# The last two weight halves of a feed-forward part's second matrix, used together, one row block after the other

## The reference, cut to what matters

```python
D_FF = 2816
def swiglu(h, w_in, w_out):
    gate, up = jnp.split(h @ w_in, 2, axis=-1)
    return (jax.nn.silu(gate) * up) @ w_out

for l in range(2):
    x = x + 0.5 * swiglu(rms_norm(x, ffa_norm[l]), ffa_w_in[l], ffa_w_out[l])
    h = rms_norm(x, mix_norm[l])
    ...                                   # three mixing branches, x = x + (...) @ w_out
    x = x + 0.5 * swiglu(rms_norm(x, ffb_norm[l]), ffb_w_in[l], ffb_w_out[l])
return x
```

## Time and profile before

| | us |
|---|---|
| median of 3 runs | 2600.22 |
| the profiled execution | 2601.14 |
| span of its trace | 2599.0 |
| TensorE busy | 2471.0 (95%) |
| GpSimd busy | 1019.3 (39%) |
| ScalarE busy | 900.9 (35%) |
| VectorE busy | 857.8 (33%) |

### The profile page before, as it was taken

How to read it: one execution, slowest core, us unless ns; L and a number is a source line. 1 busy time by engine, 2 the same in 40 slices (tenths; PEclk the granted TensorE clock), 3 DMA queues, 4 the chain that set the end, 5 groups by cost and what they waited for, 6 DMA issues and landing times. The chain is left out here.

```text
span 2599.0 us, 37017 instructions
## 1 busy us (share of the span) xinstructions
PE 2471.0 (95%) x15110; PEld 1780.1 (68%) x15110; DVE 857.8 (33%) x1424; ACT 900.9 (35%) x1342; POOL 1019.3 (39%) x428
## 2 busy tenths in 40 slices
PE   8879999999999999979999999999999999999999
PEld 3544444333443334438998899899899888998998
DVE  0332122111221122233117756421231277564211
ACT  1211211111111111134446752444444467424443
POOL 0000000000000000016887653788878876537886
PEclk9979999999999999989999999999999999999999
DMA  9139999999999999944554332555555543325554
GB/s 362 69 121 413 428 428 428 428 428 428 428 428 428 428 428 428 388 170 154 185 183 153 132 110 75 177 183 187 188 171 186 185 149 129 111 74 170 176 184 143
DMA packets 95392, 653.66 MB, mean 252 GB/s; under 512 B 10593, under 2 KB 12817, under 8 KB 69297
## 3 DMA queue, kind: packets, MB, share of 16 engines
q1 hardware_dynamic: 95280, 652.06, 65.1%
HBM read 650.96 MB, written 1.06 MB: 251 GB/s over the span
## 5 line engine op out<-in xcount | busy, mean ns | idle before, releaser
L546 POOL TENSOR_TENSOR w_lo<-raw,w_hi 128x1024 fp32r<-128x1024 f32 (+2 forms) x424 | 1019.1, 2427 | 1565.8 <-ACT w_hi L540 1565.7
L1882 PE MATMUL bank<-ring,scratch 128*64 128x512 f32 x3072 | 686.1, 596 | 29.1 <-DMA ring<-in_expert_units 26.8
L540 ACT CAST w_hi<-raw 128x1024 fp32r<-128x1024 f32 (+2 forms) x424 | 420.3, 1038 | 436.1 <-PE bank L561 428.1
L559 PE MATMUL bank<-hT_hi,w_hi 128*128 128x256 f32 x1984 | 567.3, 286 | 4.1 <-DVE hT_lo L650 4.1
L561 PE MATMUL bank<-hT_hi,w_lo 128*128 128x256 f32 x1984 | 564.2, 284 | 0.0
L560 PE MATMUL bank<-hT_lo,w_hi 128*128 128x256 f32 x1984 | 564.2, 284 | 0.0
L1882 PEld LDWEIGHTS bank<-ring,scratch 128*64 128x64 f32 x3072 | 209.6, 137 | 457.0 <-issue 386.3
L559 PEld LDWEIGHTS bank<-hT_hi,w_hi 128*128 128x128 f32 x1984 | 383.8, 193 | 6.2 <-issue 4.3
L560 PEld LDWEIGHTS bank<-hT_lo,w_hi 128*128 128x128 f32 x1984 | 383.8, 193 | 0.8
L561 PEld LDWEIGHTS bank<-hT_hi,w_lo 128*128 128x128 f32 x1984 | 383.5, 193 | 0.0
L2050 DVE TENSOR_TENSOR scratch<-bank,scratch 128x512 f32<-128x512 f32 x64 | 44.3, 692 | 606.4 <-PE bank L1896 602.5
(11 more groups left out here) (315 smaller groups left out, 2742.2 us busy)
## 6 DMA issues: line engine op xcount, KB each, us to landing
ring<-in_expert_units SPq DMA_DIRECT2D x192, 2048.0 KB, 20.6
raw<-in_layer_halves SPq DMA_DIRECT2D x408, 512.0 KB, 4.1
ring<-in_first_units SPq DMA_DIRECT2D x6, 2048.0 KB, 24.0
scratch<-in_ple_units SPq DMA_DIRECT2D x2, 2048.0 KB, 9.8
raw<-in_layer_halves SPq DMA_DIRECT2D x8, 424.0 KB, 3.3
scratch<-in_norm_gains SPq DMA_DIRECT2D x6, 512.0 KB, 6.0
raw<-in_layer_halves SPq DMA_DIRECT2D x4, 384.0 KB, 3.7
const<-in_const SPq DMA_DIRECT2D x1, 1184.0 KB, 7.5
```

What stands on the lines that cost most here:

```text
L540: k.nc.scalar.copy(k.w[0][i % SPLIT_SLOTS][:, at], k.raw[n % RAW_SLOTS][:, 0:at.stop - at.start]).then_inc(k.shared("weights_hi"), 1)
L546: k.nc.gpsimd.tensor_tensor(k.w[1][i % SPLIT_SLOTS][:, at], k.raw[n % RAW_SLOTS][:, 0:at.stop - at.start], k.w[0][i % SPLIT_SLOTS][:, at], ...
L559: nc.tensor.matmul(out, lhsT[0], rhs[0], start=start, stop=False)
L1882: last = nc.tensor.matmul(b[g * SL:(g + 1) * SL, :], lhsT[:, c, :], w[:, c, g, :], start=start and c == 0, stop=stop and c == 3)
```

## The change

For unit 5, TensorE takes the second half of out 4 ("ahead") and the half of out 5 together. For row block 0 it multiplies the two chunks of ahead into both banks, then the two chunks of out 5 into (0,0) and (0,1), each of which is released when complete; then the same for row block 1. `half_used` for ahead is raised after ahead's products for row block 1. Unit 4 does only its first half. The number of matmuls, their operands and the order of the semaphore's counts are the same.

```diff
     if u == FFN_OUT_UNITS - 1:
+        ahead = weights_pe(k, pe, (f"ffn{n}", "out", u - 1, 1), D)
         w = weights_pe(k, pe, (f"ffn{n}", "out", u, 0), D)
         for t in range(NT):
+            for i in range(2):
+                for v in range(2):
+                    last = product(ahead, 4 * u - 2 + i, i, t, v)
+            if t == 1:
+                last.then_inc(k.shared("half_used"), 1)
             for v in range(2):
                 for i in range(2):
                     last = product(w, 4 * u + i, i, t, v)
                 last.then_inc(out[t, v][1], 1)
         return
-    for h in range(2):
+    for h in range(1 if u == FFN_OUT_UNITS - 2 else 2):
         w = weights_pe(k, pe, (f"ffn{n}", "out", u, h), D)
```

## The result

The changed kernel is slower. Its median of four executions is 2620.19 us (2617.47 to 2621.55) against 2601.01 us for the kernel before; the ratio is 1.0072, 95% interval 1.0054 to 1.009, so 14 to 23 us. In a second comparison it came out at 1.0064 (1.005 to 1.0078). The forecast of 2616.7 us and its range of 2611 to 2623 hold. The profiled execution took 2619.06 us, 17.9 more than the one before.

A forecast was written before the change was run, and what follows sets the result against it. The prediction took TensorE to bound the kernel, so its standing still counts. Boundaries 12.15, program's end 1.33 and clock 3.0 sum to 16.5 us, taking the median from 2600.22 to 2616.7 us, range 2611 to 2623.

The forecast's parts named there:

- The stall: Before ahead's products, TensorE waits for act_lo of in 10: 1.33 us at each of four places, 5.3 us alone.
- the forecast's lower bound of 0.78 us: Wait before ahead's products if act_lo did not hold and only out 5's split at 1355.52 counted: 0.78 us.
- The late slot: Ahead's slot is freed later, so ScalarE's cast and the norm move 4.05 us at three boundaries, 12.15 us including the wait.
- The clock: Longer TensorE idle before the three boundaries' transposes lowers its clock: 1.6, 1.0 and 0.4 us, 3.0 in all.
- The sum: Whole program: 12.15 + 1.33 + 3.0 = 16.5 us slower, median 2616.7 us.
- The early release: VectorE takes block 0 out 1.39 us earlier, then waits for (1,0) before any variance: gain nothing.
- The rival that named the two points from which it decides: At three boundaries, early release pulls block 0's norm forward 3.2 us each: 9.5 us faster, 2590.7 us; chance 0.02.
- That only the stall counts: ScalarE's lateness is covered, boundaries move only with TensorE's wait: 4 x 1.33 = 5.3 us, 2605.5 us; chance 0.05.
- That the clock is lost at every boundary as at the start of the layers: Low TensorE clock costs 3 us at each of three boundaries: 13.5 + 3 x 3 = 22.5 us, 2622.7; chance 0.12.

The follow-up runs named there:

- the run with both mendings: Changed kernel with waits for out 5's inputs behind ahead's products for row block 0, and the second next half's cast behind block 0's squares: 1.0035.
- the second trace: The changed kernel itself, nothing altered, run and traced once more beside the experiments: 1.0064 against the kernel before.
- the run with the norm ahead: Changed kernel with waits where needed, VectorE doing block 0's variance and rows before taking out (1,0), ScalarE's cast behind block 0's root: 0.9994.
- the late release alone: Kernel before with only half_used of ahead raised 13 matmuls later: 1.0044, 11.4 us.

## Why the prediction was right

**The stall: right.** 1.33 us were forecast at each of four places. Measured from act_lo, (1,0) goes out 1.38, 1.36 and 1.36 us later, and the last piece 13.72 - 12.35 = 1.37. Alone it moves the first boundary by 1.36, and it goes when the waits move. What makes act_lo so late is itself a hold: it takes 2.45 us while GpSimd subtracts, and where GpSimd stood still the kernel before did the same instruction in

```profile
2426.98 0.69 DVE L820 TENSOR_TENSOR act_lo<-scratch,act_hi 128x512 fp32r<-128x512 f32 x1 [0.69 <-ACT act_hi L805]
```

At that length the act_lo that starts at 1353.62 would end at 1354.31, before TensorE's 1354.89; out 5's split would then have been the later input, the forecast's lower bound of 0.78 us. No run tried this.

**The late slot: right in size and in chain.** The cast starts 11.01 behind act_lo, against 6.91: 4.10 us, forecast 4.05. ScalarE became the last to arrive, L632 starts behind the squares, 3.89 us late (forecast 3.84), and by the transposes it is 4.02, 4.00 and 4.00 (forecast 4.05). That VectorE's L633 ends with GpSimd (0.02 us behind in the changed kernel) was taken up in the forecast by the rule of the Trainium skill, "SBUF — State Buffer", section "SBUF: two separate sides"; the trace agrees, and the run with both mendings shows it by itself, 1.95, 1.73 and 1.95 us at the three boundaries with nobody else late. The row of the first boundary before could not have told it, since L633 took there the 0.16 us that it takes without GpSimd too; the 0.94 us at the end of layer 0 could. The forecast used it for 0.2 us a boundary only and did not see that it also closes the obvious way of mending the cast's place.

**The clock: the right term, its parts mis-sized.** Forecast 1.6, 1.0 and 0.4 us, 3.0 in all. In the profiled execution 6.02 - 4.02 = 2.0 were measured at the first; at the end of layer 0 the marks move 4.01 us up to the next stage and 6.39 up to the next act_lo, so 2.4 behind it, at a granted clock of 0.50; at the third 23.71 - 19.37 = 4.34, so 0.3 new. That is 4.7, not 3.0. A further 0.7 of the 6.74 us up to the second act_lo came in the mixing branches behind the first boundary, in the second trace too, and isn't explained. Against it 2.3 us came back in layer 1: in this execution the norm before the second part kept its clock. The kernel before, and under it the changed one:

```profile
2404.45 1.97 PE L659 MATMUL bank<-const,h_rows 128*128 128x128 f32 x8 [2.28 <-DVE h_rows L642]
```

```profile
2423.31 1.32 PE L659 MATMUL bank<-const,h_rows 128*128 128x128 f32 x8 [2.29 <-DVE h_rows L642]
```

The kernel before had a clock of 0.59 behind it. Nothing of the change touches that place, and the second trace of the changed kernel shows that it was chance:

```profile
2420.32 1.78 PE L659 MATMUL bank<-const,h_rows 128*128 128x128 f32 x8 [2.29 <-DVE h_rows L642]
```

In that second trace the end of layer 0 has no new loss at all (4.01 us up to the next act_lo, the waits alone). The first boundary lost 2.4 us up to the split of block 1's rows, the third 2.2 up to the middle of the mixing branches, and the norm before layer 0's second part, which in the profiled execution lost nothing, some 1.1. So the single terms can't be sized from one trace, neither the forecast's nor the measured ones.

**The sum, with some luck.** 13.5 us of waits were forecast, and 3 x 4.0 + 1.4 = 13.4 measured, in both traces. With the clock 16.5 were forecast; from the first act_lo to the end the span grew by 16.6 in the profiled execution and by 19.9 in the second trace, so what is not waits took 3.2 and 6.5 us, the unexplained 0.7 among them, against the 3.0 forecast for the clock. The agreement to 0.1 us in the first is luck: its losses were larger than forecast, and the 2.3 us that came back by chance made up for them. The waits are the part that was understood.

**The early release: right.** VectorE takes block 0 out early and idles; with both orders unchanged its gain is nothing. The rival that named the two points from which it decides (cast ahead of the squares, (1,0) ahead of the variance) was what the run with the norm ahead tried; it moved block 0's variance by 3.2 us as worked out there, but only 1.1 us of this reached mla's start, since the transposes can't start before TensorE's own last product, and at the end of layer 0 only 0.3, since block 1's transposes kept their old time there (16.74 against 16.67). The 9.5 us of that rival were too much even on its own terms.

**The other rivals.** That only the stall counts is ruled out by the late release alone, 11.4 us. That the clock is lost at every boundary as at the start of the layers, 3 us each, did not happen: in the two traces a boundary lost between nothing and 2.4 us. But the 6.5 us of the second trace lie between the forecast's 3.0 and this rival's 9, so the rival was not far off in size.

## What to carry to other kernels

When products are regrouped so that one output block is done early, look at what the regrouping holds longer: the weights' slot, whose release here fed a cast at the head of another engine's queue, cost more than the stall that was easy to see (11.4 us against 3.4, each alone). Put each wait where its data are first used, not at the head of the function. Before moving a piece of work out of one engine's way, check which engine works on its result, and what that one shuts out.

## What was not expected of the hardware

VectorE's operations with two SBUF inputs stood still while a GpSimd subtraction ran: L642 took 2.66 us for two instead of 1.42, L633 up to 1.45 instead of 0.16, act_lo 2.45 instead of 0.69, while L828, with one input in PSUM, kept its 0.69 us beside it.

The low clock does not follow from the length of one idle stretch alone: 2.28 us before eight transposes was followed by it in one execution (1.97 us for the eight) and 2.29 us by the full clock in another (1.32). In both traces of the changed kernel each boundary's idle stretch, 3.55 or 4.65 us, was followed by the low clock, in the transposes or in the matmuls right after them. At the second trace's third boundary the eight transposes still ran at the full clock, and the matmuls after them at the low one:

```profile
2091.36 1.32 PE L659 MATMUL bank<-const,h_rows 128*128 128x128 f32 x8 [3.55 <-DVE h_rows L642]
2093.59 0.69 PE L559 MATMUL bank<-w_hi,hT_hi 128*128 128x424 f32 x1 [0.90 <-DVE hT_lo L650]
```

Matmuls whose results nobody reads, put into stretches of 2 us, made the kernel before 0.24% faster.
